# Twelve low weight parts made by a negated copy and an adding transfer instead of a subtraction

## What is computed

```
def second_block(x, ...):
    for l in range(DEPTH):                      # DEPTH = 2
        h = rms_norm(x, norm_mix_g[l])
        p = h @ w_in[l]
        ...                                     # convolution, attention, gated linear attention
        x = x + y
        h = rms_norm(x, norm_ffn_g[l])
        u = causal_depthwise_conv(h @ ffn_w_up[l], ffn_conv_w[l], ffn_conv_b[l])   # 3 taps, 2 * 2816 columns
        x = x + (silu(u[..., :D_FF]) * u[..., D_FF:]) @ ffn_w_down[l]
    return rms_norm(x, final_g)
```

## Time and profile before

| | us |
|---|---|
| time, median of 3 runs (lowest, highest) | 1216.2 (1215.86, 1216.25) |
| profiled execution: span from the first to the last instruction | 1214.1 |
| TensorE busy in it | 1205.5 |
| VectorE busy | 903.9 |
| ScalarE busy | 671.1 |
| GpSimd busy | 51.3 |

### The profile page before, as it was taken

The page is one execution under the profiler, slowest core; times in us unless marked ns, Lnnn a source line. Parts: engine busy times, 40 slices in busy tenths (PEclk is TensorE's granted clock), DMA queues, the critical chain, the costliest instruction groups (busy, mean ns, idle before and its releaser), DMA issues.

```text
span 1214.1 us, 17930 instructions
## 1 busy us (share of the span) xinstructions
PE 1205.5 (99%) x7099; PEld 1048.0 (86%) x7099; DVE 903.9 (74%) x1105; ACT 671.1 (55%) x807; POOL 51.3 (4%) x101
## 2 busy tenths in 40 slices
PE   9999999999999999999999999999999999999998
PEld 7888888888899888888888889999888888999986
DVE  5566465568886685566988986988887998698886
ACT  7655354445466664444648556555655755566553
POOL 2000000000010000000010020000001011000000
PEclk9999999999999999999999999999999999999999
DMA  9644645545654335554555454455574435555550
GB/s 349 232 164 168 223 147 200 194 163 196 243 191 166 131 141 206 207 179 168 193 214 174 139 177 161 152 205 174 174 262 161 140 107 184 191 179 180 196 196 35
DMA packets 32568, 220.40 MB, mean 182 GB/s; under 512 B 3888, under 2 KB 4048, under 8 KB 6768
## 3 DMA queue, kind: packets, MB, share of 16 engines
q1 hardware_dynamic: 29888, 212.33, 49.3%
q0 software_dynamic: 1664, 5.41, 1.3%
q10 hardware_dynamic: 944, 1.64, 0.4%
HBM read 218.31 MB, written 1.05 MB: 181 GB/s over the span
## 4 chain that ended last, share of the span: by engine, by line
PE 92%; DVE 6%; DMA 1%; issue 0%; POOL 0%; ACT 0%; ACTq 0%; POOLq 0%; DVEq 0%
PE acc L1850 20%; PE acc L1852 20%; PE acc L1851 20%; PE tb L1878 3%; PE tb L2521 3%; PE tb L2520 3%; PE acc L2520 3%; PE acc L2521 3%; PE tb L2518 3%; PE acc L2518 3%; DVE cacc L1534 3%; DVE wlo L1143 1%; PE acc L2158 1%; PE acc L2160 1%; PE acc L2161 1%; PE tb L1850 1%
## 5 line engine op out<-in xcount | busy, mean ns | idle before, releaser
L1143 DVE TENSOR_TENSOR wlo<-raw,whi 128x2048 fp32r<-128x2048 f32 x184 | 417.3, 2287 | 131.8 <-ACT whi L592 131.8
L592 ACT ACTIVATE whi<-raw 128x2048 fp32r<-128x2048 f32 (+1 forms) x198 | 368.4, 1882 | 56.5 <-PE acc L1852 43.9
L1850 PE MATMUL acc<-whi,xth 128*128 128x512 f32 x704 | 279.8, 397 | 0.6 <-DVE xtl L1241 0.5
L1852 PE MATMUL acc<-whi,xtl 128*128 128x512 f32 x704 | 274.7, 390 | 0.0
L1851 PE MATMUL acc<-wlo,xth 128*128 128x512 f32 x704 | 274.3, 390 | 0.0
L1850 PE MATMUL acc<-whi,yth 128*128 128x512 f32 (+1 forms) x428 | 169.0, 395 | 0.0
L1852 PE MATMUL acc<-whi,ytl 128*128 128x512 f32 (+1 forms) x428 | 166.6, 389 | 0.0
L1851 PE MATMUL acc<-wlo,yth 128*128 128x512 f32 (+1 forms) x428 | 166.4, 389 | 0.0
L1850 PEld LDWEIGHTS acc<-whi,xth 128*128 128x128 f32 x704 | 132.3, 188 | 28.0 <-DVE wlo L1232 1.3
L1852 PEld LDWEIGHTS acc<-whi,xtl 128*128 128x128 f32 x704 | 132.2, 188 | 28.1
L1851 PEld LDWEIGHTS acc<-wlo,xth 128*128 128x128 f32 x704 | 132.4, 188 | 25.7
(11 more groups left out here) (407 smaller groups left out, 1919.3 us busy)
## 6 DMA issues: line engine op xcount, KB each, us to landing
raw<-in_stream SPq DMA_DIRECT2D x200, 1024.0 KB, 5.0
rb<-in_rel_rows POOLq DMA_DIRECT2D x8, 256.0 KB, 2.9
x<-in_x_in ACTq DMA_DIRECT2D x4, 256.0 KB, 7.4
raw<-in_stream SPq DMA_DIRECT2D x2, 512.0 KB, 9.3
gs_sb<-in_gs_row POOLq DMA_DIRECT2D x1, 1024.0 KB, 7.6
frow<-in_fin_row POOLq DMA_DIRECT2D x2, 512.0 KB, 6.0
raw<-in_stream SPq DMA_DIRECT2D x2, 256.0 KB, 7.0
ws_sb<-in_ws_t POOLq DMA_DIRECT2D x1, 512.0 KB, 7.7
```

The costliest lines, as they stand in the source:

```text
L592: act.activation(whi[:, s, c0:UNIT], raw[:, s, c0:UNIT], ACT.Copy).then_inc(hi_ready, 1)
L1143: dve.tensor_tensor(wlo[:, s, :], raw[:, s, :], whi[:, s, :], ALU.subtract).then_inc(lo_ready, 1)
L1850: pe.matmul(o, xh, wh, start=first, stop=False)
L1852: return pe.matmul(o, xl, wh, start=False, stop=last)
```

## The change

For 12 units the low part is made in another way. They are the second units of steps 5 to 10 (`FAR_STEPS`) of the up stage of both layers, gathered in the list `FAR`. ScalarE, right after `whi` of such a unit, writes `wlo = -1 * raw`, rounded as before, which is the negated high part, and raises `neg_ready`. GpSimd waits for that and for the landing of its previous transfer of this kind, and issues a transfer that reads the unit from the stream in HBM once more and adds it onto `wlo`; when it has landed, `far_landed` rises by 16. VectorE skips these units. TensorE waits for `far_landed` in place of `lo_ready` there, and SP loads the next unit into such a slot on `neg_ready`. Since `lo_ready` now counts fewer units, SP's loop ends at the first of the far units and the later issues are written out one by one. Some semaphores that GpSimd used once for its own steps are merged into one, `pool_step`, which changes no instruction.

```
+FAR_STEPS = (5, 6, 7, 8, 9, 10)
...
+        FAR = [gu(l) + 15 + 2 * j + 1 for l in range(2) for j in FAR_STEPS]
+
+        def lo_count(U):
+            return U + 1 - sum(f <= U for f in FAR)
+
+        def far_count(U):
+            return FAR.index(U) + 1
+
+        def wait_lo(eng, U, t=0):
+            if U in FAR:
+                eng.wait_ge(far_landed, 16 * far_count(U))
+            else:
+                eng.wait_ge(lo_ready, lo_count(U) + 4 * t)
...
-            groups = TOTAL // SLOTS - 1
+            groups = FAR[0] // SLOTS
...
             for u in range(SLOTS * (groups + 1), TOTAL):
-                sp.wait_ge(lo_ready, u - SLOTS + 1)
+                if u - SLOTS in FAR:
+                    sp.wait_ge(neg_ready, far_count(u - SLOTS))
+                else:
+                    sp.wait_ge(lo_ready, lo_count(u - SLOTS))
                 sp.dma_start(raw[:, u % SLOTS, :], stream[u]).then_inc(raw_ready[u % SLOTS], 16)
...
+                for j in FAR_STEPS:
+                    U = gu(l) + 15 + 2 * j + 1
+                    pool.wait_ge(neg_ready, far_count(U))
+                    if U != FAR[0]:
+                        pool.wait_ge(far_landed, 16 * far_count(U) - 16)
+                    pool.dma_start(wlo[:, U % SLOTS, :], stream[U], accum_op=ALU.add).then_inc(far_landed, 16)
...
                 act.activation(whi[:, s, c0:UNIT], raw[:, s, c0:UNIT], ACT.Copy).then_inc(hi_ready, 1)
+                if U in FAR:
+                    act.activation(wlo[:, s, :], raw[:, s, :], ACT.Copy, scale=-1.0).then_inc(neg_ready, 1)
...
             def lo(U, t=0):
 
-                if U >= TOTAL:
+                if U >= TOTAL or U in FAR:
                     return
...
                     for half in range(2):
                         s = (U1 + 2 * j + half) % SLOTS
-                        pe.wait_ge(lo_ready, U1 + 2 * j + half + 1)
+                        wait_lo(pe, U1 + 2 * j + half)
```

More of the change, by code:

```diff
@@ L249, in two_blocks_kernel @@
         hi_ready, lo_ready, unit_used = sem("hi_ready"), sem("lo_ready"), sem("unit_used")
+        neg_ready, far_landed = sem("negated_hi_ready"), sem("added_lo_landed")
         m0_done, out_group = sem("m0_done"), sem("out_group")
@@ L258, in two_blocks_kernel @@
             sem(n) for n in ("consts_loaded", "consts_made", "made"))
-        n_add, n_tr, n_gm, n_hi, n_lo, n_sq, n_ms, n_r = (
-            sem("norm_" + n) for n in ("added", "transposed", "gained", "hi", "lo", "squared", "meaned", "rms"))
+        n_add, n_tr, n_gm, n_hi, n_lo, n_sq, n_r = (
+            sem("norm_" + n) for n in ("added", "transposed", "gained", "hi", "lo", "squared", "rms"))
         x2_z, x2_hi, x2_lo = sem("second_x_scaled"), sem("second_x_hi"), sem("second_x_lo")
@@ L263, in two_blocks_kernel @@
         f_ms, f_rt = sem("final_meaned"), sem("final_rms")
-        side_made, x_r2 = sem("side_made"), sem("mix_own_rms")
-        a_ev, a_vsq, a_vsum, a_ms, a_r, a_vn, a_sp, a_spc, a_y, y_banks, a_hi, a_lo = (
-            sem("gmlp_" + n) for n in ("act", "v_squared", "v_summed", "v_meaned", "v_rms", "v_normed", "spatial",
+        side_made, pool_step = sem("side_made"), sem("pool_own_step")
+        a_ev, a_vsq, a_vsum, a_r, a_vn, a_sp, a_spc, a_y, y_banks, a_hi, a_lo = (
+            sem("gmlp_" + n) for n in ("act", "v_squared", "v_summed", "v_rms", "v_normed", "spatial",
                                        "spatial_kept", "gated", "turned_then_sums_done", "hi", "lo"))
@@ L283, in two_blocks_kernel @@
             sem("conv_" + n) for n in ("padded", "sigmoid", "gated", "transposed", "kept", "tap"))
-        x_ltr, x_bn, x_ag, x_lms, x_lr, x_nrm, x_btr, x_sl = (
-            sem("conv_ln_" + n) for n in ("transposed", "stats", "mean", "var", "rstd", "normed", "back", "silu"))
+        x_ltr, x_bn, x_ag, x_lr, x_nrm, x_btr, x_sl = (
+            sem("conv_ln_" + n) for n in ("transposed", "stats", "mean", "rstd", "normed", "back", "silu"))
         x_ev = sem("mix_kept")
@@ L459, in _, with then_wait @@
                                pattern=[[-GCH, P // GCH], [0, GCH]], channel_multiplier=1).then_inc(consts_made, 1)
+            steps = [0]
+            def then_wait(op):
+                steps[0] += 1
+                op.then_inc(pool_step, 1)
+                pool.wait_ge(pool_step, steps[0])
             def root(r, outer=None):
                 pool.wait_ge(n_sq, 2 * r + 2)
-                pool.tensor_scalar(ssq(r, 0, 2), ssq(r, 0, 2), 1.0 / D, EPS, ALU.mult, ALU.add).then_inc(n_ms, 1)
-                pool.wait_ge(n_ms, r + 1)
+                then_wait(pool.tensor_scalar(ssq(r, 0, 2), ssq(r, 0, 2), 1.0 / D, EPS, ALU.mult, ALU.add))
                 two = stat[:, 2 * r:2 * r + 2]
@@ L468, in root @@
                 if outer is not None:
-                    last.then_inc(x_r2, 1)
-                    pool.wait_ge(x_r2, 1)
+                    then_wait(last)
                     last = pool.tensor_tensor(two, two, stat[:, 2 * outer:2 * outer + 2], ALU.mult)
@@ L503, in _ @@
             pool.wait_ge(a_vsum, 1)
-            pool.tensor_scalar(stat[:, 66:68], stat[:, 64:66], 1.0 / DFF_A, EPS, ALU.mult, ALU.add).then_inc(a_ms, 1)
-            pool.wait_ge(a_ms, 1)
+            then_wait(pool.tensor_scalar(stat[:, 66:68], stat[:, 64:66], 1.0 / DFF_A, EPS, ALU.mult, ALU.add))
             pool.tensor_tensor(stat[:, 68:70], stat[:, 66:68], mhalf[:, 0:2], ALU.pow).then_inc(a_r, 1)
@@ L550, in _ @@
                 pool.wait_ge(x_ag, 2 * l + 2)
-                pool.tensor_scalar(stat[:, 72:74], mvv[:, :, 1], 1.0, LN_EPS, ALU.mult, ALU.add).then_inc(x_lms, 1)
-                pool.wait_ge(x_lms, l + 1)
+                then_wait(pool.tensor_scalar(stat[:, 72:74], mvv[:, :, 1], 1.0, LN_EPS, ALU.mult, ALU.add))
                 pool.tensor_tensor(stat[:, 74:76], stat[:, 72:74], mhalf[:, 0:2], ALU.pow).then_inc(x_lr, 1)
@@ L592, in hi @@
                 act.activation(whi[:, s, c0:UNIT], raw[:, s, c0:UNIT], ACT.Copy).then_inc(hi_ready, 1)
+                if U in FAR:
+                    act.activation(wlo[:, s, :], raw[:, s, :], ACT.Copy, scale=-1.0).then_inc(neg_ready, 1)
             def sums_hi(e, i):
                 f, h, _ = w_sums(e, i)
-                act.wait_ge(lo_ready, down_at(e) + sevens(e)[i] + 1)
+                act.wait_ge(lo_ready, lo_count(down_at(e) + sevens(e)[i]))
                 act.activation(h[:, :], f[:, :], ACT.Copy).then_inc(side_hi, 1)
@@ L1860, in in_group @@
                     if m == 0:
-                        pe.wait_ge(lo_ready, U + half + 1 + 4 * t)
+                        wait_lo(pe, U + half, t)
                     if norm is not None:
@@ L1898, in seven @@
                 w = [slice(512 * b, 512 * b + 512) for b in range(4)]
-                pe.wait_ge(lo_ready, U + j + 1)
+                wait_lo(pe, U + j)
                 ready(j)
@@ L2150, in kq_step @@
                     s = (U_KVQ + 2 * j + half) % SLOTS
-                    pe.wait_ge(lo_ready, U_KVQ + 2 * j + half + 1)
+                    wait_lo(pe, U_KVQ + 2 * j + half)
                     for f in range(4):
@@ L2269, in k_step @@
                 def k_step(hooks={}):
-                    pe.wait_ge(lo_ready, U0 + 3)
+                    wait_lo(pe, U0 + 2)
                     pe.wait_ge(x_gl, l + 1)
```

## The result

| | before | change |
|---|---|---|
| time, median (lowest, highest), us | 1216.03 (1215.77, 1216.25), 4 runs | 1235.41 (1234.7, 1238.88), 4 runs |
| ratio, 95% interval | | 1.0165 (1.0151 to 1.0179) |
| profiled execution: time, span | | 1234.7, 1233.0 |

The sign was right and the time lies at the upper end of the range, but the forecast was 1220.6. (The weight stream has 202 units, not the 204 of the kernel's description above; no number hangs on it.)

A forecast was written before the change was run, and what follows sets the result against it. TensorE, idle for 8.6 of 1214.1 us, was taken as the bound. A 9.5 us transfer against 7.3 us of room gave 2.2 us of stall in each of two layers: 1216.2 + 4.4 = 1220.6 us, range 1215.5 to 1236.

The forecast's parts named there:

- The duration L: Time from GpSimd's issue of an adding transfer to its landing, taken as 9.5 us.
- Two reads, 5.9 us: Within the transfer's time: reading 1 MB from HBM and 1 MB of `wlo` one after the other, 5.9 us.
- Fixed, 2.0 us: Within the transfer's time: a fixed part of about 2.0 us, taken from a plain 1 MB load.
- An interleaved load, 1.6 us: Within the transfer's time: half of a weight load served between its rows, 1.6 us.
- The upper bound by bytes, 10.9 us: Transfer's highest time by bytes: 2.0 us fixed, 5.9 for both reads, 3.0 for one whole load.
- second rival: Up stage: transfers become the bound, each waiting for the previous landing, if one takes over 11.5 us; much slower, chance 0.20.
- VectorE will only be idle more: Removing twelve VectorE subtractions, 27.4 us in all, was costed at 0 because nobody on the path waits for them.
- The clock: A TensorE stall can also cost clock; mean 0.67 in 5 us of idleness at the end, none shown for 2 us.
- The room of 7.3 us: Step 5, each layer: time from the negated copy's end at 789.35 to the unit's need at 796.7.
- Step 7's room of 11.3: Step 7: negated copy ends at 808.4, unit needed at 819.7, so room 11.3 us and no stall.
- No gain from VectorE's lighter load: VectorE's lighter load was not expected to speed TensorE's matmuls; that rival's price 1.2 us, any gain over 0.2% chance 0.04.
- the chained transfers: Up stage, six transfers a layer: at 12.5 us each, first stall 5.2, then about 1.0 at five steps; 1236.4 us, chance 0.20.

The follow-up runs named there:

- experiment 2: The changed kernel with the GpSimd transfer as a plain copy, without the addition (output changed): 1226.13 us, ratio 1.0085 to the kernel before.
- experiment 4: The changed kernel with only step 10's unit made the new way: 1227.64 us; the same with loads held until the transfer landed: 1217.71 us.
- experiment 7: The changed kernel with throwaway matmuls ahead of TensorE's wait at step 5 of each layer: 1234.07 us with 40, 1236.92 us with 60.
- experiment 1: The changed kernel without the transfer: ScalarE's negated copies and SP's written-out issues stay, VectorE subtracts over them; 1215.77 us, ratio 1.0001 to before.
- experiment 5: The changed kernel with far units at steps 7 to 10 only: 1231.0 us, ratio 1.0127 to the kernel before.
- experiment 6: The changed kernel with negated copy and transfer for columns 1024 to 2047 only, VectorE subtracting the others: 1216.63 us, ratio 1.0006 to before.

## Why the prediction had the sign and not the size

**The step that failed is "The duration L".** I took 9.5 us; the first transfers took 12.6 and about 13. Term by term:
- *Two reads, 5.9 us:* right. Measured 5.4 us of all engines against 2.7 for a plain transfer (experiment 2). The Trainium skill's page "Collectives: The Full Stack", in "The bandwidth ceiling: the fold count and why AG ≠ RS ≠ AR", has a reducing transfer read two sources and run at half the rate of a copy. The trace agrees.
- *Fixed, 2.0 us:* 8.2 alone less 5.4 is 2.8 (experiment 4). 0.8 short.
- *An interleaved load, 1.6 us:* this was the large miss. At step 5 it is 12.6 - 8.2 = 4.4 us; at the other steps, by the median, 3.0. I had counted half of one load. In fact 2.80 MB of loads ran in these 13 us, and the engines were full from 791 on, with the stream's queue at 55% and the transfer's at 40%. My sentence that loads "give way" was wrong: the load that left at 789.34 landed at 801.83, ahead of the transfer, which landed at 802.22. The upper bound by bytes, 10.9 us, let only one load in between.

**The loads were there to be counted.** The trace of before has 2.83 MB of loads in the same 13 us, since the stage loads two units in every 11.52 us. The prediction used this in its second rival, where two loads and a transfer ask the engines for 11.8 us in each step, "so they are full", but not in L. A side of the change that I had costed at nothing also moved loads: "VectorE will only be idle more" missed that SP waits for VectorE. Together with the wait on `neg_ready`, which I did see, it moved two issues forward by 2.4 and 4.1 us. How much this order cost, no run shows; it did not add to the amount.

**The clock.** I named it in a rival and put nothing for it in the sum. It cost 1.8 and 2.1 us behind the two long stalls, 3.9 us in all. Over all runs of this document, each of the thirteen stalls of this stage that lasted 2.3 us or longer was followed by matmuls at the 0.50 level, and none of those under 1.8 us. Of the six between 1.8 and 2.2 us three were (1.9, 2.0 and 2.1) and three were not (1.9, 2.0 and 2.2), so that the length alone does not tell. The 48 matmuls behind a fall took 1.4 to 2.8 us more. The Trainium skill's page "TensorE: Matmul & The Clock Gate", in "What's actually happening", says that an idle array falls back to half rate. The trace agrees for the long stalls, and experiment 7 shows full clock where the array is kept busy.

**The sum with these numbers.** First layer: 12.6 + 0.3 (from the copy's end to the issue) - 7.3 = 5.6 us, 1.8 of clock, 1.8 of a chained transfer at step 8: 9.2 of 9.46 us. Hence 4.4 us became 18.9.

**What held.** The room of 7.3 us (789.31 to 796.64). ScalarE's copies and SP's issues at 0 (experiment 1). The rooms of steps 6 to 10: only waits of 0.2 to 1.6 us there. Step 7's room of 11.3 depends on steps 5 and 6 being far units (experiment 5). No gain from VectorE's lighter load (experiments 1 and 6).

**The rivals.** Of the chained transfers half is true: for five of the ten later units it was the previous landing that ended GpSimd's wait, and one transfer, step 8's, took 12.8 us and brought the stall of 1.6 us. But once the first stall has shifted TensorE, later transfers take about 11 us and nearly fit its 11.5, so the expected microsecond at each step did not come. That rival's 1236.4 is near the result by luck: its first stall was right (5.2), but its five further ones of about 1.0 were in truth one of 1.6 in the first layer, 0.5 us in the second, and the clock.

**Open:** how the 16 engines divide their time between two queues; what the earlier loads alone cost; why the landing grew to 14.2 us in the kernel with 40 filling matmuls; and what decides on the clock behind a stall of about 2 us.

No version beats the kernel before, and none could by this way: TensorE is idle for 8.6 us there and for none of it in this stage.

## What to carry to other kernels

Work moved off an engine for which nobody waits can only cost, so price the new path against the room that its first use has, not its average one. A transfer's length is the one beside the loads that run with it: 8.2 us alone was 10.1 to 13.1 here. Read the bytes that the other queues already move in the new transfer's window from the trace of before, and add their engine time to its own. Look at whose issues the relieved engine releases. Allow for a lower clock behind a stall of TensorE: it cost 1.4 to 2.8 us behind every one of 2.3 us or longer, and behind some of about 2 us.

## What was not expected of the hardware

The addition inside a transfer costs as much engine time as a second read (5.4 against 2.7 us for 1 MB) and makes GpSimd's issue 0.86 to 0.97 us long, where that of the plain transfer takes 0.53 to 0.63. Plain loads and an adding transfer shared the 16 engines with 55% for the loads, and the transfer grew by 3 us at the median and 4.4 in the first layer's step 5. One of 512 KB landed in 5.8 us at the median (11.2 for 1 MB) and in 8.1 at step 5 (12.6).
